# Reordering the first loads and splits, and the last squares and output tiles, of a hybrid RG-LRU and attention block in three-product fp32

## Chip, cores and metric

One core of one Trainium2 chip. The metric is the device time of one execution in microseconds; shorter is better. Three runs of the kernel before gave a median of 1032.5 us (1031.96 to 1032.81).

## What is computed

One layer on 1024 tokens of width 1024, in float32. Cut to what matters:

```python
h = rmsnorm(x, g_mix); z = h @ w_in                # 1024 x 1024 @ 1024 x 1792
lx, lg, q, k, v = split(z)
lx = causal_depthwise_conv(lx, w_conv, b_conv)
y_lru = rmsnorm(rg_lru(lx, ...) * gelu(lg), g_lru_out)
y_att = rmsnorm(chunk_window_attention(q, k, v, sinks), g_attn_out)
x = x + concatenate([y_lru, y_att]) @ w_out
x = x + square(relu(rmsnorm(x, g_ffn) @ w_ff1)) @ w_ff2     # width 4096
gate = sigmoid(rmsnorm(x, g_ple) @ w_ple_gate)
x = x + gate * (p @ w_ple_proj)
return rmsnorm(x, g_final)
```

## The kernel before

Everything is held transposed: channels on the 128 partitions, tokens along the free axis. xT is x as eight tiles of 128 channels (k = 0 to 7) by 1024 tokens, worked in two halves of 512 tokens (`half(0)`, `half(1)`). Each float32 operand of a matrix product is split into a rounded part (hi, made by ScalarE as a copy to fp32r) and a remainder (lo, by VectorE or GpSimd as a subtraction), and each product is three matmuls in a row, hi x hi (L815), lo x hi (L816), hi x lo (L817). The order of instructions is written out by hand for each engine, and semaphores join them. A wait stops its engine's whole queue.

**The head.** w_in is read in pieces of [2, 128, 1024]; a half piece `s` holds four k tiles of 256 columns. The first half piece (s = 0) is loaded in two parts: columns 0 to QP = 512 (L495, k = 0 and 1) and QP to HP = 1024 (L497, k = 2 and 3). SP issues, in this order: the first part (L495), the vectors (gains and biases, [128, 80], L496), the second part (L497), token tiles 2 and 3 (L499), then the half pieces s = 1, 2, 3 (L488) with pairs of token tiles (L481) between and behind them. ScalarE's own queue issues token tiles 0 and 1 (L1216, L1217) and then waits for constants and data. Semaphores: tile 0 `first_x_in`, tile 1 `x_in[0]`, tile 2 `x_in[1]`, tile 3 `third_x_in`, the second part `stage_in[0]`.

Splitting: VectorE makes h_hi of tile 0 (L1774, needs the vectors and tile 0), w_lo of the first part (L1776), h_lo of tiles 0 and 1 (`mix_low`, recorded at L1682), w_lo of the second part (L1785), h_lo of tile 2, the first sum of squares, h_lo of tile 3, and w_lo of s = 1 (L1691). ScalarE makes w_hi of the first part (L1221), h_hi of tile 1 (`mix_high`, recorded at L1192), w_hi of the second part (L1239), h_hi of tile 2, the square of tile 0 (L1197), h_hi of tile 3, w_hi of s = 1 (L1178), and so on. TensorE runs nine warming products (L968), then `first_half`: k = 0 in three steps of two columns blocks each (L846, L850, L854), k = 1 (needs h_lo of tile 1), k = 2 and 3 (need the second part's w_lo and their h_lo), then s = 1, 2, 3 in turn. Six matmuls belong to each k: two column blocks by three. The second token half follows from group 4 on, with the sums of squares (L881, L882) in the middle of its first group.

**The tail.** The last stage works in 20 cells (`CELLS`), q = 0 to 19: eight channel tiles by token parts, the last ones 256 tokens wide. For each, TensorE multiplies the gate (`gate`) and projects (`project`, both L815 to L817); VectorE multiplies by the norm (`gate_scale`, L2255), ScalarE takes the sigmoid (L1610), VectorE multiplies by the projection and adds to x (`gate_add`, L2269 and L2271), ScalarE squares (`final_square`, L1617), GpSimd sums (L798). Cells come in pairs; step q = 16 is cells 16 and 17, step 18 is cells 18 and 19. Between them VectorE writes finished output tiles, `out_tile(k, part)` at L2275 (part 0 is 512 tokens, parts 1 and 2 are 256 each; part 2 is the last), and SP stores them in pairs of k, waiting in order. For the last part ScalarE loads the table of the square root early by a tiny operation (L1640), squares cell 18 (`final_square(q - 1)`), scales tile 6 (`final_scale`, L1626), and takes two roots of column sums (L1651). TensorE's column sums (L1151) stand behind seven warming products (L1154) and read the running sum, the square of cell 18 and that of cell 19 (VectorE, L2314). Then VectorE inverts (L2319), makes two diagonals (L2322), TensorE spreads them (L1166), and the last tiles are multiplied (L2329, L807) and stored (L681, L1659).

Of the kernel before, what the change touches and what calls it, by code (L numbers as in the profile page):

```python
# [13 lines left out]
P = 128  # L14
SEQ = 1024
D = 1024
KD = D // P
# [102 lines left out]
def build(nc, x, p, vectors, gates_w, w_in, w_out, w_ff1, w_ff2, w_ple_gate, w_ple_proj, alibi, out):  # L120
    ctx = ExitStack()
    with ctx:
# [3 lines left out]
        def at(name, offset, shape, dt=F32):  # L126
            return nc.alloc_sbuf_tensor_at(name, shape, dt, offset=base + offset)

        def sem(name):
            return ctx.enter_context(nc.semaphore(name))  # L130
# [5 lines left out]
        xT = at("xT", XT, [P, KD, SEQ])  # L136
# [81 lines left out]
        for name, shape in (("r_mix", [P, SEQ]), ("ident", [P, P]), ("ones", [P, P]), ("vec", [P, NVEC]),  # L218
# [7 lines left out]
        r_mix, ident, ones, vec = (small[n] for n in ("r_mix", "ident", "ones", "vec"))  # L226
# [11 lines left out]
        x_in = [sem(f"x_in{i}") for i in range(8)]  # L238
        stage_in = [sem(f"stage_in{i}") for i in range(STAGES)]

        vec_in, gatew_in, bias_in, p_in = sem("vec_in"), sem("gatew_in"), sem("bias_in"), sem("p_in")
        pw_in, pw_high, pw_ready, pp_kept = sem("pw_in"), sem("pw_high"), sem("pw_ready"), sem("pp_kept")
        last_square = sem("last_square")
        first_w_in, first_x_in, third_x_in, last_done = (
            sem(n) for n in ("first_w_in", "first_x_in", "third_x_in", "last_done"))
# [44 lines left out]
        def half(hf):  # L290
            return slice(hf * HALF, (hf + 1) * HALF)
# [185 lines left out]
        def _(sp):  # L477
# [15 lines left out]


            sp.dma_start(stage[:, 0, 0:QP], w_in[0, 0, :, 0:QP]).then_inc(first_w_in, 16)  # L495
            sp.dma_start(vec[:, :], vectors).then_inc(vec_in, 16)  # L496
            sp.dma_start(stage[:, 0, QP:HP], w_in[0, 0, :, QP:HP]).then_inc(stage_in[0], 16)  # L497
            for k in (2, 3):
                sp.dma_start(xT[:, k, half(0)], x[k * P:(k + 1) * P, half(0)]).then_inc(  # L499
                    x_in[1] if k == 2 else third_x_in, 16)  # L500
            for s in range(1, 4):
                if s > 1:
                    load_x(s)
# [167 lines left out]
            for part in range(LAST):  # L671
                for pair in range(KD // 2):
                    k = 2 * pair
# [497 lines left out]
        def _(act):  # L1171
# [37 lines left out]
            def root(n, b, dst, width):  # L1209
# [3 lines left out]
                act.activation(dst[:, tok], bank[b][:, 0:cols], ACT.Sqrt, bias=eps[:, 0:1],  # L1213
                               scale=1.0 / width).then_inc(rms_done, 1)

            act.dma_start(xT[:, 0, half(0)], x[0:P, half(0)]).then_inc(first_x_in, 16)  # L1216
            act.dma_start(xT[:, 1, half(0)], x[P:2 * P, half(0)]).then_inc(x_in[0], 16)  # L1217
            act.wait_ge(consts, 3)
            act.activation(lam[:, 2, :], ones[:, 0:LT], ACT.Square)
            act.wait_ge(first_w_in, 16)  # L1220
# [3 lines left out]
            def mix_high(k, hf):  # L1224

                if (k % 2 == 0) if hf or k > 1 else (k == 1):
                    act.wait_ge(x_in[4 * hf + k // 2], 16)
                if hf == 0 and k == 3:
                    act.wait_ge(third_x_in, 16)
                split_high(H_MIX + KD * hf + k, xT[:, k, half(hf)], v_mix[:, k:k + 1], k, hf)  # L1230

            def mix_square(k, hf):

                square(KD * hf + k, sq, xT[:, k, half(hf)])

            act.wait_ge(h_high, H_MIX + 1)
            mix_high(1, 0)
            act.wait_ge(stage_in[0], 16)
            act.activation(w_hi[:, 0, QP:HP], stage[:, 0, QP:HP], ACT.Copy).then_inc(w_high, 1)  # L1239
            mix_high(2, 0)  # L1240
            mix_square(0, 0)
            mix_high(3, 0)
            high(1)
# [333 lines left out]
            def gate_high(n):  # L1577

                high(2 * n)
                high(2 * n + 1)  # L1580
# [31 lines left out]
            def final_square(q):  # L1612

                m, _, tok, _ = cell(q)
                act.wait_ge(x_gated, 2 * (q + 1))
                act.wait_ge(sq_used, SQ_BY[SS_FIN - 1] + q - 1)
                act.activation(cell_square(q), xT[:, m, tok], ACT.Square).then_inc(sq_done, 1)  # L1617
# [10 lines left out]
            for q in range(len(CELLS)):  # L1628
                if q in (14, 17):
                    root(SS_FIN + (q == 17), 4, r_fin, D)  # L1630
                sigmoid(q)
                if q == 0:
                    total_head(SS_PLE + 1)
                if q == 3:
                    root(SS_PLE + 1, 4, r_mix, D)
                if q in (5, 7):
                    act.wait_ge(gate_done, q + 1)
                    gate_high(GATE_FIRST + 2 + (q == 7))
                if q == len(CELLS) - 1:
                    act.activation(lam[:, 2, :], ones[:, 0:LT], ACT.Sqrt)  # L1640
                    final_square(q - 1)
                    final_scale(KD - 2)
                elif q % 2 == 1:
                    final_square(q - 1)
                    final_square(q)
                if 16 <= q < 19:
                    for k in (2 * (q - 16), 2 * (q - 16) + 1):
                        final_scale(k)
# [15 lines left out]
        def _(dve):  # L1664
# [113 lines left out]
            def mix_low(k, hf):  # L1778

                split_low(H_MIX + KD * hf + k, xT[:, k, half(hf)], v_mix[:, k:k + 1], k, hf)  # L1780

            mix_low(0, 0)
            mix_low(1, 0)
            dve.wait_ge(w_high, 1)
            dve.tensor_tensor(w_lo[:, 0, QP:HP], stage[:, 0, QP:HP], w_hi[:, 0, QP:HP], ALU.subtract  # L1785
                              ).then_inc(w_split, 1)
            mix_low(2, 0)
            add_square(dve, SS_MIX, 0, sq, acc)
            mix_low(3, 0)
            w_low(1)  # L1790
# [482 lines left out]
            def out_tile(k, part):  # L2273

                dve.scalar_tensor_tensor(out=result(k, part), in0=xT[:, k, tokens(part)], scalar=v_fin[:, k:k + 1],  # L2275
                                         in1=r_fin[:, tokens(part)], op0=ALU.mult, op1=ALU.mult
                                         ).then_inc(out_ready[k], 1)

            for q in range(0, len(CELLS), 2):
                gate_scale(q)  # L2280
                if q == 0:
                    for i in range(6, KD):
                        ple_low(i, 1)
                if q == 14:
                    invert(SS_FIN, r_fin)
                if q == 16:
                    for k in (2, 3, 4):
                        out_tile(k, 0)
                if q == 18:
                    for k in (6, 7):  # L2290
                        out_tile(k, 0)
                    for k in (0, 1):
                        out_tile(k, 1)
                gate_scale(q + 1)
                if q == 16:
                    invert(SS_FIN + 1, r_fin)
                gate_add(q)
                gate_add(q + 1)
                if q == 2:
                    invert(SS_PLE + 1, r_mix)  # L2300
                if q in (4, 6):
                    for h in range(2):
                        w_low(2 * (GATE_FIRST + 2 + (q == 6)) + h)
                if q == 14:
                    for k in (0, 1):
                        out_tile(k, 0)
                if q == 16:
                    out_tile(5, 0)

            q = len(CELLS) - 1  # L2310
# [1 line left out]
            dve.wait_ge(x_gated, 2 * (q + 1))  # L2312
            dve.wait_ge(sq_used, SQ_BY[SS_FIN - 1] + q - 1)
            dve.tensor_tensor(cell_square(q), x_last, x_last, ALU.mult).then_inc(last_square, 1)  # L2314
            for k in range(2, KD - 2):
                out_tile(k, 1)
            dve.wait_ge(rms_done, SS_FIN + LAST + LAST_HALVES)
            columns = lam[:, 3, 0:LAST_HALVES]
# [70 lines left out]
```

## Time and profile before

| | us |
|---|---|
| median of three runs | 1032.5 (1031.96 to 1032.81) |
| the profiled execution | 1032.53 |
| its span | 1030.7 |
| TensorE matmul busy | 1021.3 (99%) |
| VectorE busy | 765.9 (74%) |
| ScalarE busy | 526.5 (51%) |
| GpSimd busy | 500.1 (49%) |

The span is the time between the first and the last instruction or transfer of the profile; the execution's own time is 1.8 us more. Busy shares are of the span. TensorE's granted clock is 0.998 of full over the span. Times in the rows below are microseconds from the span's start.

### The profile page before, as it was taken

What the parts mean: (1) busy time and instruction counts of PE and PEld (TensorE: products, weight loads), DVE (VectorE), ACT (ScalarE), POOL (GpSimd) and SP (SyncE); (2) the same over time, 40 slices, a digit from 0 to 9 for tenths busy, and PEclk for the clock granted to TensorE, in tenths of its full rate; (3) what the DMA queues carried; (4) which work ended last, traced back from release to release, by engine and by line L of the source; (5) the groups of instructions that cost most, each with busy time, mean ns of one, the idle gap of its engine ahead of it and who ended that gap; (6) DMA issues with size and microseconds to landing.
All of it is one profiled execution on the core that took longest, in us unless ns stands there. A gap on an engine that the chain in (4) does not pass through costs nothing.

```text
span 1030.7 us, 13984 instructions
## 1 busy us (share of the span) xinstructions
PE 1021.3 (99%) x4780; PEld 836.0 (81%) x4780; DVE 765.9 (74%) x906; ACT 526.5 (51%) x940; POOL 500.1 (49%) x350
## 2 busy tenths in 40 slices
PE   9999999999999999999999999999999999999997
PEld 7877788777888788888888888888888888888897
DVE  7988787888798777787787787866776765754658
ACT  7557755655677534334334355443455453653334
POOL 0000052343304887887887657445557555741221
PEclk9999999999999999999999999999999999999999
DMA  9101102102003666767867699668985664600004
GB/s 346 44 26 57 41 0 93 41 10 69 6 1 133 248 236 249 273 245 259 280 240 260 242 350 325 194 215 286 313 262 175 192 198 150 220 1 1 1 1 164
DMA packets 63972, 166.15 MB, mean 161 GB/s; under 512 B 6960, under 2 KB 9008, under 8 KB 61872
## 3 DMA queue, kind: packets, MB, share of 16 engines
q1 hardware_dynamic: 63088, 164.43, 46.2%
q10 hardware_dynamic: 832, 1.05, 0.3%
q8 instruction: 30, 0.49, 0.2%
q14 instruction: 22, 0.18, 0.1%
HBM read 115.12 MB, written 50.33 MB: 161 GB/s over the span
## 4 chain that ended last, share of the span: by engine, by line
PE 92%; DVE 5%; issue 1%; ACT 1%; DMA 1%; SPq 0%; DVEq 0%; ACTq 0%
PE bank L815 30%; PE bank L816 29%; PE bank L817 29%; PE bank L930 1%; PE bank L960 1%; DVE h_lo L1984 1%; PE bank L901 1%; PE bank L945 1%; DVE r_ffn L1696 1%; DMA stage<-in_w_in 1%; DVE t_lo L2076 0%; DVE acc L465 0%; ACT t_hi L1475 0%; PE bank L885 0%; DVE w_lo L1691 0%
## 5 line engine op out<-in xcount | busy, mean ns | idle before, releaser
L815 PE MATMUL bank<-h_hi,w_hi 128*128 128x512 f32 (+1 forms) x574 | 220.9, 385 | 0.6 <-DVE h_lo L1682 0.5
L816 PE MATMUL bank<-h_lo,w_hi 128*128 128x512 f32 (+1 forms) x574 | 217.0, 378 | 0.0
L817 PE MATMUL bank<-h_hi,w_lo 128*128 128x512 f32 (+1 forms) x574 | 216.9, 378 | 0.0
L773 POOL TENSOR_TENSOR left_lo<-left_raw,left_hi 128x512 fp32r<-128x512 f32 x88 | 125.7, 1436 | 104.7 <-ACT left_hi L1531 104.1
L2153 DVE TENSOR_TENSOR right_lo<-right_raw,right_hi 128x512 fp32r<-128x512 f32 x88 | 117.4, 1347 | 56.7 <-ACT right_hi L1532 56.6
L815 PE MATMUL bank<-right_hi,left_hi 128*128 128x512 f32 x352 | 136.9, 389 | 0.0
L817 PE MATMUL bank<-right_hi,left_lo 128*128 128x512 f32 x352 | 136.9, 389 | 0.0
L816 PE MATMUL bank<-right_lo,left_hi 128*128 128x512 f32 x352 | 136.9, 389 | 0.0
L815 PEld LDWEIGHTS bank<-h_hi,w_hi 128*128 128x128 f32 x574 | 108.0, 188 | 28.9 <-issue 6.2
L817 PEld LDWEIGHTS bank<-h_hi,w_lo 128*128 128x128 f32 x574 | 108.0, 188 | 20.4
L816 PEld LDWEIGHTS bank<-h_lo,w_hi 128*128 128x128 f32 x574 | 108.1, 188 | 19.6 <-issue 0.5
L1531 ACT ACTIVATE left_hi<-left_raw 128x512 fp32r<-128x512 f32 x88 | 55.5, 631 | 111.2 <-DMA right_raw<-u_b 62.9
L745 POOL TENSOR_TENSOR slot_lo<-w_raw,slot_hi 128x512 fp32r<-128x512 f32 x56 | 78.6, 1405 | 24.0 <-ACT slot_hi L1494 23.7
L815 PE MATMUL bank<-h_hi,slot_hi 128*128 128x512 f32 x224 | 87.7, 392 | 0.9 <-DVE u L2114 0.9
L2089 DVE TENSOR_TENSOR w_set<-w_set 128x512 f32<-128x512 f32 x52 | 76.2, 1465 | 14.9 <-DMA w_set<-in_w_ff 14.0
L817 PE MATMUL bank<-h_hi,slot_lo 128*128 128x512 f32 x224 | 87.2, 389 | 0.0
L816 PE MATMUL bank<-h_lo,slot_hi 128*128 128x512 f32 x224 | 87.2, 389 | 0.0
L817 PEld LDWEIGHTS bank<-right_hi,left_lo 128*128 128x128 f32 x352 | 66.1, 188 | 13.8
L815 PEld LDWEIGHTS bank<-right_hi,left_hi 128*128 128x128 f32 x352 | 66.1, 188 | 13.8
L816 PEld LDWEIGHTS bank<-right_lo,left_hi 128*128 128x128 f32 x352 | 66.1, 188 | 13.6
L745 POOL TENSOR_TENSOR slot_lo<-s_raw,slot_hi 128x512 fp32r<-128x512 f32 x42 | 60.1, 1446 | 20.2 <-ACT slot_hi L1494 18.3
L817 PE MATMUL bank<-t_hi,slot_lo 128*128 128x512 f32 x168 | 65.4, 389 | 0.0
(250 smaller groups left out, 2031.9 us busy)
## 6 DMA issues: line engine op xcount, KB each, us to landing
w_raw<-in_w_ff SPq DMA_DIRECT2D x28, 512.0 KB, 5.4
right_raw<-u_b SPq DMA_DIRECT2D x56, 256.0 KB, 4.3
w_set<-in_w_ff SPq DMA_DIRECT2D x26, 512.0 KB, 5.9
w_sums<-w_set SPq DMA_DIRECT2D x13, 1024.0 KB, 3.9
left_raw<-w_sums SPq DMA_DIRECT2D x48, 256.0 KB, 3.9
left_raw<-in_w_ff SPq DMA_DIRECT2D x40, 256.0 KB, 3.0
u_b<-u SPq DMA_DIRECT2D x16, 512.0 KB, 3.0
u_t<-usq SPq DMA_DIRECT2D x16, 512.0 KB, 6.4
```

The source lines that it names most:

```text
L745: pool.tensor_tensor(slot_lo[i], w1_left(raw, i), slot_hi[i], ALU.subtract).then_inc(w1_split, 1)
L773: pool.tensor_tensor(left_lo[o][:, :], left_raw[o][:, :], left_hi[o][:, :], ALU.subtract).then_inc(left_ready, 1)
L815: pe.matmul(o, whi, hh, start=first, stop=False, skip_group_check=onto)
L816: pe.matmul(o, whi, hl, start=False, stop=False, skip_group_check=onto)
L817: return pe.matmul(o, wlo, hh, start=False, stop=last, skip_group_check=onto)
L901: last = pe.matmul(bank[4 + 2 * hf + i][gate_block(i, n), :], gate_w[block, i, j, block], yl(j)[block, half(hf)], start=True, stop=True)
L930: last = pe.matmul(bank[4 + g][:, (2 * cp + a) * P:(2 * cp + a + 1) * P], qT[r, c, 2 * a:2 * a + 2, :].rearrange("p a q -> p (a q)"), kT[r ...
L945: last = pe.transpose(bank[6 + g][:, i * P:(i + 1) * P], prob[:, u % 2, (4 * g + i) * P:(4 * g + i + 1) * P], ident[:, :])
L960: last = pe.matmul(bank[3][g * HD:(g + 1) * HD, cp * 256:(cp + 1) * 256], v[:, c, g * HD:(g + 1) * HD], probT[:, g * 512 + cp * 256:g * 51 ...
L1531: act.activation(left_hi[o][:, :], left_raw[o][:, :], ACT.Copy).then_inc(left_high, 1)
L2089: dve.tensor_tensor(out, one, other, op).then_inc(made, 1)
L2153: dve.tensor_tensor(right_lo[o][:, :], right_raw[o][:, :], right_hi[o][:, :], ALU.subtract).then_inc(right_ready, 1)
```

## The change

Four moves. The count of operations, transfers and bytes stays.

1. The vectors' load goes from SP's second place to the first place of ScalarE's queue. Token tile 0 is second there. Token tile 1 moves to SP's second place, and tile 2 to SP's third, ahead of the second part of the first half piece, which is now fourth; tile 3 stays fifth.
2. ScalarE rounds tile 2 ahead of the second part of the weights, and VectorE makes tile 2's remainder ahead of that part's.
3. The square of cell 18 stands ahead of the operation that loads the square root's table.
4. Of the output tiles, tile 6 of part 0 moves from step 18 to step 16, and tile 2 of part 1 from behind the last square to step 18.

```diff
--- before.py
+++ after.py
@@ -493,11 +493,10 @@
 
 
             sp.dma_start(stage[:, 0, 0:QP], w_in[0, 0, :, 0:QP]).then_inc(first_w_in, 16)
-            sp.dma_start(vec[:, :], vectors).then_inc(vec_in, 16)
+            for k, arrived in ((1, x_in[0]), (2, x_in[1])):
+                sp.dma_start(xT[:, k, half(0)], x[k * P:(k + 1) * P, half(0)]).then_inc(arrived, 16)
             sp.dma_start(stage[:, 0, QP:HP], w_in[0, 0, :, QP:HP]).then_inc(stage_in[0], 16)
-            for k in (2, 3):
-                sp.dma_start(xT[:, k, half(0)], x[k * P:(k + 1) * P, half(0)]).then_inc(
-                    x_in[1] if k == 2 else third_x_in, 16)
+            sp.dma_start(xT[:, 3, half(0)], x[3 * P:4 * P, half(0)]).then_inc(third_x_in, 16)
             for s in range(1, 4):
                 if s > 1:
                     load_x(s)
@@ -1213,8 +1212,8 @@
                 act.activation(dst[:, tok], bank[b][:, 0:cols], ACT.Sqrt, bias=eps[:, 0:1],
                                scale=1.0 / width).then_inc(rms_done, 1)
 
+            act.dma_start(vec[:, :], vectors).then_inc(vec_in, 16)
             act.dma_start(xT[:, 0, half(0)], x[0:P, half(0)]).then_inc(first_x_in, 16)
-            act.dma_start(xT[:, 1, half(0)], x[P:2 * P, half(0)]).then_inc(x_in[0], 16)
             act.wait_ge(consts, 3)
             act.activation(lam[:, 2, :], ones[:, 0:LT], ACT.Square)
             act.wait_ge(first_w_in, 16)
@@ -1235,9 +1234,9 @@
 
             act.wait_ge(h_high, H_MIX + 1)
             mix_high(1, 0)
+            mix_high(2, 0)
             act.wait_ge(stage_in[0], 16)
             act.activation(w_hi[:, 0, QP:HP], stage[:, 0, QP:HP], ACT.Copy).then_inc(w_high, 1)
-            mix_high(2, 0)
             mix_square(0, 0)
             mix_high(3, 0)
             high(1)
@@ -1637,8 +1636,8 @@
                     act.wait_ge(gate_done, q + 1)
                     gate_high(GATE_FIRST + 2 + (q == 7))
                 if q == len(CELLS) - 1:
+                    final_square(q - 1)
                     act.activation(lam[:, 2, :], ones[:, 0:LT], ACT.Sqrt)
-                    final_square(q - 1)
                     final_scale(KD - 2)
                 elif q % 2 == 1:
                     final_square(q - 1)
@@ -1781,10 +1780,10 @@
 
             mix_low(0, 0)
             mix_low(1, 0)
+            mix_low(2, 0)
             dve.wait_ge(w_high, 1)
             dve.tensor_tensor(w_lo[:, 0, QP:HP], stage[:, 0, QP:HP], w_hi[:, 0, QP:HP], ALU.subtract
                               ).then_inc(w_split, 1)
-            mix_low(2, 0)
             add_square(dve, SS_MIX, 0, sq, acc)
             mix_low(3, 0)
             w_low(1)
@@ -2284,12 +2283,11 @@
                 if q == 14:
                     invert(SS_FIN, r_fin)
                 if q == 16:
-                    for k in (2, 3, 4):
+                    for k in (2, 3, 4, 6):
                         out_tile(k, 0)
                 if q == 18:
-                    for k in (6, 7):
-                        out_tile(k, 0)
-                    for k in (0, 1):
+                    out_tile(7, 0)
+                    for k in (0, 1, 2):
                         out_tile(k, 1)
                 gate_scale(q + 1)
                 if q == 16:
@@ -2312,7 +2310,7 @@
             dve.wait_ge(x_gated, 2 * (q + 1))
             dve.wait_ge(sq_used, SQ_BY[SS_FIN - 1] + q - 1)
             dve.tensor_tensor(cell_square(q), x_last, x_last, ALU.mult).then_inc(last_square, 1)
-            for k in range(2, KD - 2):
+            for k in range(3, KD - 2):
                 out_tile(k, 1)
             dve.wait_ge(rms_done, SS_FIN + LAST + LAST_HALVES)
             columns = lam[:, 3, 0:LAST_HALVES]
```

## Rows read from the trace of the kernel before

**Rows 1.** The page, part 4: shares of the chain that ended last, by engine.
```profile
PE 92%; DVE 5%; issue 1%; ACT 1%; DMA 1%; SPq 0%; DVEq 0%; ACTq 0%
```

**Rows 2.** TensorE's waits in the whole span: in total, times, longest us.
```profile
PE bank L815 <- DVE u L2114: 0.9, 1, 0.9
```

**Rows 3.** Chain that ended last, 0 to 13 us: start, us, what.
```profile
1.68 5.56 DMA stage<-in_w_in
...
7.27 0.64 ACT w_hi L1239
...
7.93 0.69 DVE w_lo L1785
...
8.64 0.76 DVE h_lo L1682
...
9.54 0.47 PE bank L815
10.02 0.23 PE bank L816
```

**Rows 4.** DMA issues, one at a time: KB each, us from issue to landing.
```profile
xT<-in_x ACTq DMA_DIRECT2D x1, 256.0 KB, 3.6
...
vec<-in_vectors SPq DMA_DIRECT2D x1, 40.0 KB, 3.7
...
xT<-in_x ACTq DMA_DIRECT2D x1, 256.0 KB, 4.4
...
stage<-in_w_in SPq DMA_DIRECT2D x1, 256.0 KB, 5.6
...
stage<-in_w_in SPq DMA_DIRECT2D x1, 512.0 KB, 6.7
```

**Rows 5.** DMA view, 0 to 14 us: rate in 40 slices of 0.35 us.
```profile
GB/s 0 0 0 0 0 82 222 380 363 365 369 259 190 193 176 228 298 375 421 398 392 421 410 415 392 386 369 351 357 369 415 427 404 386 421 421 433 427 392 392
```

**Rows 6.** Timeline of the two issuing queues: start, us, queue, line, transfer.
```profile
1.20 0.46 ACTq L1217 DMA_DIRECT2D xT<-in_x  x1
...
2.15 0.91 SPq L499 DMA_DIRECT2D xT<-in_x  x2
```

**Rows 7.** Timeline, 4 to 13 us: start, us, engine, line, out<-in, [idle before <-releaser].
```profile
4.92 0.49 DVE L1774 TENSOR_SCALAR h_hi<-xT,vec 128x512 fp32r<-128x512 f32 x1 [3.90 <-DMA vec<-in_vectors]
...
5.92 1.41 DVE L1682 SCALAR_TENSOR_TENSOR h_lo<-xT,vec,h_hi 128x512 fp32r<-128x512 f32 x2
...
9.85 1.06 ACT L1178 ACTIVATE w_hi<-stage 128x1024 fp32r<-128x1024 f32 x1
...
11.02 1.23 DVE L1691 TENSOR_TENSOR w_lo<-stage,w_hi 128x1024 fp32r<-128x1024 f32 x1 [0.49 <-ACT w_hi L1178]
...
12.37 0.43 PE L815 MATMUL bank<-h_hi,w_hi 128*128 128x512 f32 x1
```

**Rows 8.** VectorE's timeline, and the chain (TensorE), where k = 7 nears.
```profile
32.02 0.73 DVE L1682 SCALAR_TENSOR_TENSOR h_lo<-xT,vec,h_hi 128x512 fp32r<-128x512 f32 x1
...
33.95 0.23 PE bank L817
```

**Rows 9.** Chain that ended last, from 1019 us on: start, us, what.
```profile
1020.24 1.56 PE bank L1154 x14
1021.80 1.15 PE bank L1151 x10
...
1022.97 0.48 ACT lam L1651 x2
```

**Rows 10.** Timeline of VectorE and ScalarE, 1020 to 1023 us; columns as in rows 7.
```profile
1020.14 0.42 DVE L2271 TENSOR_TENSOR xT<-xT,gt 128x256 f32<-128x256 f32 x1
...
1020.25 1.28 ACT L1640 ACT_TABLE_LOAD   x1
...
1021.65 0.40 ACT L1617 ACTIVATE sq<-xT 128x256 f32<-128x256 f32 x1
1022.09 0.51 ACT L1626 ACTIVATE xT<-xT,vec 128x256 f32<-128x256 f32 x1
```

**Rows 11.** VectorE's timeline in step 18: two long and two short output tiles.
```profile
1017.10 2.35 DVE L2275 SCALAR_TENSOR_TENSOR xT<-xT,vec,r_fin 128x512 f32<-128x512 f32 x4
```

## The prediction

> **What bounds the kernel now.** I read the page first: the chain that ended last lies on TensorE for 92% of the span, on VectorE for 5% [rows 1]. The kernel is a stream of matrix products that hardly ever stops. So I asked for TensorE's waits in the whole span: after the first 10 us the only ones that the view names are 0.9 us in the feed-forward part, which is fed by TensorE's own products [rows 2], and one in the last 8 us. Whatever the change gains must come from before the stream is dense or from behind its end, where the edits lie. It can be worth tenths of a microsecond.
>
> The head is read in the chain of its first 13 us [rows 3]. The chain is: the load of the second piece (columns QP to HP of the first half of w_in's first piece), issued at 1.68 and landed at 7.24; ScalarE's rounding, 0.64; VectorE's remainder, 0.69; VectorE's h_lo of token tile 2, 0.76; TensorE at 9.54. Both tile 2 and the piece are needed for the products of k = 2. TensorE then runs k = 2 and 3 (twelve products at 0.23) and meets a second gate: the next half piece, L1178 to L1691, lets it go on at 12.37 [rows 7]. From there it runs through.
>
> The tail is TensorE's too: seven warming products (14 records), the column sums, and only then ScalarE's two roots at 1022.97 [rows 9].
>
> **The head, part by part.** Call H the start of VectorE's first operation, L1774, which needs the vectors and token tile 0. It is 4.92, and the vectors are what it waited for [rows 7]. Behind it VectorE runs without a gap to the end of h_lo of tile 1 at 5.92 + 1.41 = 7.33, which is H + 2.41 [rows 7]. TensorE's six products of k = 1 take 0.47 + 5 x 0.23 = 1.62 [rows 3]. So TensorE could begin k = 2 at H + 4.05 = 8.97 with 0.02 for the hand-over, and begins at 9.54: **0.57 us is the stall that the second piece causes**.
>
> 1. Order of tile 2 and the piece. Tile 2's rounding (ScalarE) and h_lo (VectorE) go ahead of the piece. If both have landed in time, VectorE's chain ends at 7.33 + 0.76 + 0.69 = 8.78 for the old H, below 8.97: the stall goes, and what is late next is VectorE's chain from H itself. The edit puts ScalarE's wait for tile 2 ahead of the piece's rounding; queued behind it are that rounding, L1197 and tile 3. TensorE needs both before k = 2, so a late tile costs the difference between it and the piece only.
>
> 2. Queues. SP issues every 0.47 us. Its second place goes from the vectors (40 KB) to tile 1, the third from the piece to tile 2, the fourth (2.15 [rows 6]) to the piece, the fifth stays with tile 3. ScalarE's queue has the vectors at 0.75 and tile 0 at 1.20, the place that tile 1 had [rows 6]. Issue counts stay, and GpSimd's instructions and queue are untouched. The vectors took 3.7 from issue, so they land near 0.75 + 3.7 = 4.45, and H now hangs on tile 0. Bounds: it took 3.6 when it was first in the queue, giving 4.8; tile 1, second in the same queue behind a full tile, took 4.4, giving 5.6 [rows 4]. Tile 0 will stand second, but behind 40 KB instead of 256 KB, so I take 5.05 as an estimate between them: **H is 0.13 later**.
>
> 3. The next half piece. It is the fifth load behind the first of SP and took 6.7 us from its issue [rows 4]; ScalarE takes it at 9.85, and TensorE gets it 2.52 us later, at 12.37 [rows 7]. All that is ahead of it is the same number of bytes, so the question is how well the DMA engines are filled. The rate line has a hollow: six slices of 0.35 us (from 3.85 us on) at 259 to 298, while later ones stand near 390 GB/s [rows 5]. The hollow misses (131 + 200 + 197 + 214 + 162 + 92) x 0.35 us = 0.35 MB, or 0.9 us at 390 GB/s. It begins when the vectors are being written through SP's queue, and the load behind them took 5.6 where those ahead took 3.6 [rows 4]. If small rows in SP's queue make the hollow, SP's stream is free of it now and the half piece comes up to 0.9 earlier; if the hollow is only the start of the DMA engines, nothing moves. I take about half, 0.5: forecast landing 9.3 where it was 9.83.
>
> **The Trainium skill beside it.** The trace shows the load behind the vectors landing 2.34 us after them (7.24 against 4.90). The skill's page "DMA: Bandwidth & Descriptors" (Specifications) wants transfers of at least 512 B for the line rate; a row of the vectors is 80 numbers, 320 B. By that rule the small rows, now ahead of tile 0 in one queue, slow what stands behind them; that is the third rival, priced from rows below.
>
> **The sum.** TensorE passes the second gate at the later of H + 4.05 + 12 x 0.228 = H + 6.79 and the half piece's handling + 2.52. With H = 5.05 the first is 11.84; with a landing at 9.3 (taken up 0.02 later, as before) the second is 11.84 as well. Against 12.37 the gain is **0.53 us**. It must survive to the end. The nearest thing behind the gate is k = 7 of group 4: VectorE's h_lo is done at 32.75, TensorE wants it at 34.18 [rows 8], a slack of 1.4, more than the gain even if VectorE does not move. Behind that every wait of TensorE is for work that its own products started, so it shifts along.
>
> **The tail.** The out tiles: one long one (512 columns) goes from step 18 to step 16, where it fills an idle stretch before TensorE's next result, and a short one (tile 2 of part 1) comes from behind the last square to step 18. Four tiles, two long and two short, took 2.35 [rows 11], that is 0.39 for 256 columns, so VectorE reaches its last gate_scale 0.39 earlier. Its next operation needs TensorE's projection, which ends 6 products of 0.12 before 1020.24, at 1019.52, so the last adds come 0.1 to 0.2 earlier. ScalarE: the square of cell 18 waits for the add that ended at 20.56 (1020.14 + 0.42 [rows 10]). It then runs 0.40, the table 1.28, the small root (0.12 to the next start) and the scaling (0.51) [rows 10]: 1020.60 + 0.40 + 1.28 + 0.12 + 0.51 = 1022.91 at the old time of the add, 1022.75 with the earlier add. The root is wanted at 1022.97, when TensorE's tenth column record ends. TensorE is busy without a gap from 1020.24 until then [rows 9], and its two reads of that square follow one another; so neither the earlier square nor the tile taken from behind the last square shortens anything: **0.0**, bounds -0.1 (the square was just in time at 22.05 and may have held one record) and +0.1 (the margin of 0.06 is used up). What hides the moved table is TensorE's warming and sums; without that cover its 1.28 would count. The stores of part 1 leave up to 0.4 earlier, but the last store hangs on the roots.
>
> Forecast: the profiled execution took 1032.53 with a span of 1030.7, so 1.8 us lie around it; it equals the median of 1032.5. 1032.53 - 0.53 = **1032.0**.
>
> **Rivals.**
> - A. The places hold: each load lands when the load in its place did. The piece, at 2.15, lands 5.6 later at 7.75, is rounded and split (0.64 + 0.69) by 9.1; TensorE may start k = 2 0.3 earlier, but the half piece is where it was and gives it all back at 12.37. Time 1032.5. For it: from 5.6 us on the rate is full, so landing goes by bytes. Against: the hollow.
> - B. Slower: tile 0 is late behind the vectors. The load behind the vectors landed 2.34 us after them. Applied to ScalarE's queue: 4.45 + 2.34 = 6.8 = H, the gate opens at 13.6, **+1.2**: 1033.7. It turns to a loss from H = 5.58 on. Against it: the hollow may be of both queues, and tile 0 is the only load there, while the piece had SP's stream and tile 1 beside it.
> - C. The tail gives too: if the last square's reads did hold TensorE, or the stores' earlier end frees the last ones, 0.3 more: 1031.7.
> - D. The table. In the trace ScalarE's load of the root's table takes 1.28 and the next operation begins 0.01 later [rows 10]. The skill's page "ScalarE: Activation LUTs" (What ACT_TABLE_LOAD costs) adds a drain of about 1.38 us to each switch. As a mechanism of this kernel: an added pause as long as the load itself (1.28) behind it would put the roots at 22.91 + 1.28 = 24.2, +1.2: 1033.7. The rows leave no room for it before the change (21.53 to 21.65), so 0.01.
>
> **How the numbers follow.** Forecast 0.46 (its own range 1031.6 to 1032.3), A 0.28, B 0.13, C 0.07, D 0.01, and 0.05 for something that the trace doesn't show (a different meeting of DMAs in the streamed part), half of it either way. The three runs lie 0.85 apart, so 0.3 of noise is added at both ends. From C's 1031.7 and a landing 0.9 earlier (H at 4.8: 0.78) down, 1031.2; up to A with noise, 1032.9; left out are most of B, D and the unknown. A measurement of this kernel can tell about 0.2%, 2.1 us, from no change. No named case reaches that: same 0.94, faster 0.03, slower 0.03, all from the unknown and its like.
>
> **What would show it.** Right: L1774 released by tile 0 at 5.0 to 5.2; tile 2's h_lo ahead of the piece's remainder; no wait of 0.5 on h_lo before 10 us; the half piece's rounding near 9.3; the first product behind the second gate near 11.8; in the tail ScalarE idle for 0.0 to 0.2 before the roots and TensorE's last sums as long after its last projection as now. Wrong: L1774 after 5.6 (B); L1178 still at 9.85 (A); the roots earlier relative to the projections (C); a pause behind the table (D); a difference of over 2 us, which would have to appear in the streamed part.

## The result, and the profile after

The changed kernel took 1033.78 us (median of 22 runs, 1032.63 to 1035.83), the kernel before 1032.2 (22 runs, 1031.79 to 1032.96) beside it. The ratio is 1.0014, with a 95% interval of 1.0008 to 1.0019: **1.6 us slower** where 0.5 faster was forecast, and above the stated range. By the bound of 0.2% it is still no change. The spread grew from 1.2 to 3.2 us. The times stand in groups: 8 runs up to 1033.2 (median 1032.87), 10 from 1033.7 to 1034.3, 4 from 1034.5 on.

The profiled execution took 1033.83 (before 1032.53), its span is 1032.0 (before 1030.7). The shares of the chain hardly moved against [rows 1]:

```profile
PE 92%; DVE 5%; ACT 1%; issue 1%; DMA 0%; ACTq 0%; DVEq 0%
```

The head tells it. Timeline of the changed kernel, 0 to 14 us (start, us, engine, line, out<-in, idle before and its releaser); it answers to [rows 6, 7]:

```profile
1.14 4.21 PE L967 MATMUL bank<-ones 128*128 128x128 f32 x18 [1.14 <-POOL eps L690]
1.20 0.90 SPq L497 DMA_DIRECT2D xT<-in_x  x2
1.21 0.45 ACTq L1216 DMA_DIRECT2D xT<-in_x  x1
...
6.14 0.49 DVE L1773 TENSOR_SCALAR h_hi<-xT,vec 128x512 fp32r<-128x512 f32 x1 [5.13 <-DMA xT<-in_x]
...
6.78 1.19 PE L845 MATMUL bank<-h_hi,w_hi 128*128 128x512 f32 x2 [1.43 <-DVE h_hi L1773]
...
9.47 0.63 PE L814 MATMUL bank<-h_hi,w_hi 128*128 128x512 f32 x1
...
9.62 1.04 ACT L1177 ACTIVATE w_hi<-stage 128x1024 fp32r<-128x1024 f32 x1
...
9.90 0.52 PE L815 MATMUL bank<-h_lo,w_hi 128*128 128x512 f32 x1
10.26 0.39 PE L816 MATMUL bank<-h_hi,w_lo 128*128 128x512 f32 x1
...
13.93 0.39 PE L814 MATMUL bank<-h_hi,w_hi 128*128 128x512 f32 x1
```

Token tile 0 releases VectorE's first operation at 6.14; before, the vectors released it at 4.92. TensorE, whose warming products end at 5.35, sits idle for 1.43 us, and when it starts, its products lie 0.43 apart (9.47, 9.90) until about 10.2, and 0.23 after that; before, they were 0.23 apart from k = 1 on. The product behind the second gate (the wait for the next half piece of w_in) starts at 13.93 instead of 12.37: 1.56 late. The half piece was not in the way, its rounding began at 9.62.

The DMA issues one at a time (KB, us from issue to landing), which answer to [rows 4]:

```profile
vec<-in_vectors ACTq DMA_DIRECT2D x1, 40.0 KB, 3.3
...
xT<-in_x SPq DMA_DIRECT2D x1, 256.0 KB, 4.7
...
xT<-in_x ACTq DMA_DIRECT2D x1, 256.0 KB, 4.8
...
stage<-in_w_in SPq DMA_DIRECT2D x1, 256.0 KB, 5.4
```

The vectors land at 4.05, tile 1 (SP's second) at 5.9, tile 0 (ScalarE's second) at 6.05, the second weight part at 7.5.

The tail, which answers to [rows 9, 10]. First TensorE's closing warming products in the timeline of the kernel before:

```profile
1020.08 1.73 PE L1154 MATMUL bank<-ones 128*128 128x128 f32 x14
```

Then those of the changed kernel, and ScalarE behind them:

```profile
1021.50 1.73 PE L1153 MATMUL bank<-ones 128*128 128x128 f32 x14
...
1021.96 0.42 ACT L1616 ACTIVATE sq<-xT 128x256 f32<-128x256 f32 x1 [0.58 <-DVE xT L2270]
1022.39 1.28 ACT L1640 ACT_TABLE_LOAD   x1
1023.69 0.20 ACT L1640 ACTIVATE lam<-ones 128x4 f32<-128x4 f32 x1
1023.80 0.49 ACT L1625 ACTIVATE xT<-xT,vec 128x256 f32<-128x256 f32 x1
1024.27 0.48 ACT L1650 ACTIVATE lam<-bank,eps 128x1 f32<-128x1 f32 x2
```

ScalarE now runs from the square to the roots without a gap. The roots begin 2.77 us after the first closing warming product (1021.50 to 1024.27), before 2.89 (1020.08 to 1022.97): **the tail gained 0.12**.

### The profile page after: what moved, and what is told of

Read it like the earlier page. It is cut to its first block, busy times and chain, and to the rows that moved or that the text cites. A ratio compares the mean times of both kernels' runs of the same rounds, so it can differ in the third digit from the quotient of the medians.

```text
span 1032.0 us, 13984 instructions
## 1 busy us (share of the span) xinstructions
PE 1021.9 (99%) x4780; PEld 837.4 (81%) x4780; DVE 766.0 (74%) x906; ACT 526.0 (51%) x940; POOL 499.4 (48%) x350
## 4 chain that ended last, share of the span: by engine, by line
PE 92%; DVE 5%; ACT 1%; issue 1%; DMA 0%; ACTq 0%; DVEq 0%
PE bank L814 30%; PE bank L815 29%; PE bank L816 29%; PE bank L929 1%; PE bank L959 1%; DVE h_lo L1983 1%; PE bank L900 1%; PE bank L944 1%; DVE r_ffn L1695 1%; DMA xT<-in_x 0%; DVE t_lo L2075 0%; DVE acc L465 0%; ACT t_hi L1474 0%; PE bank L884 0%; DVE w_lo L1690 0%
```

## The experiments

Theory at this point: (1) tile 0 is late because it stands second in ScalarE's queue, behind the vectors; (2) the idle stretch of TensorE costs as much again through its clock; (3) the tail is a small gain. The rival to (1) is that SP's full tiles in the first microseconds make ScalarE's loads late, whatever their order; the rival to (2) is that lateness is all.

### Head and tail apart

`tail_only` is the kernel before with the tail's hunks of the diff alone; `head_only` is the changed kernel with these undone.

```diff
                 if q == len(CELLS) - 1:
+                    final_square(q - 1)
                     act.activation(lam[:, 2, :], ones[:, 0:LT], ACT.Sqrt)
-                    final_square(q - 1)
...
-                    for k in (2, 3, 4):
+                    for k in (2, 3, 4, 6):
                         out_tile(k, 0)
...
-            for k in range(2, KD - 2):
+            for k in range(3, KD - 2):
```

> The kernel before with the tail's edits alone (square of cell 18 ahead of the table, the two output tiles moved). In the changed kernel's profile TensorE's first read of that square starts 0.36 us after the sums' start where it was 0.47 before, and ScalarE is the last to be ready. Theory (the tail gives 0.1): roots begin 0.1 us earlier relative to the end of the last projection, time 0.1 below the kernel before. Rival (the tail costs, because the table now stands behind the square): roots 0.1 or more later. If the whole loss came from the tail, this kernel would be 1.5 slower.

Measured: 1031.91 (11 runs) against 1032.27, ratio 0.9996 (0.9987 to 1.0005). Its profile:

```profile
1019.57 1.73 PE L1154 MATMUL bank<-ones 128*128 128x128 f32 x14
...
1022.34 0.49 ACT L1651 ACTIVATE lam<-bank,eps 128x1 f32<-128x1 f32 x2
```

2.77 us again. The 0.12 is in both profiles with this tail; the time, 0.36 lower, agrees in sign but its interval holds zero.

> The changed kernel with the tail of before. Theory (the head costs all of it: token tile 0, second in ScalarE's queue behind the vectors, lands near 6.0 and TensorE starts 1.2 us later, at half its clock until near 10): 1.6 to 1.7 us slower than the kernel before, with runs spread over 2 us or more. Rival (head and tail disturb each other): no slower than 1.0.

Measured: 1034.12 against 1032.27, ratio 1.0013 (1.0004 to 1.0022), 1032.77 to 1034.7. The head costs all of it. The profiled execution was one of the quick group, 1032.80: VectorE's first operation at 6.01, TensorE idle for 1.29, and yet its products were 0.23 apart from the start of k = 1 on, and the roots came 2.89 after the warming, as before. So lateness and slow products are two things. (The expectation had put slow products into this profile; they were not in it.)

### Is the slow stretch the clock, and what is it worth?

```diff
-WARM, WARM_END = 9, 7
+WARM, WARM_END = 12, 7
```

> The changed kernel with 12 warming products instead of 9, which keeps TensorE busy until 6.6 us, about when its first operand is there. Theory (two costs: 0.5 to 0.6 for the late token tile, 1.0 for products at half the clock after the idle 1.4 us): full clock from near 5.7 us on, second gate near 12.9 where it was 13.9, time 1.0 below the changed kernel, 0.4 to 0.5 above the kernel before. Rival (the clock costs nothing of its own, the lateness is all): as the changed kernel.

Measured: 1032.89 against 1032.27 for the kernel before, ratio 1.0006 (0.9997 to 1.0015); ten of eleven runs lie between 1032.64 and 1033.09. With this the upper groups are gone but for one run. Profile:

```profile
6.27 0.49 DVE L1773 TENSOR_SCALAR h_hi<-xT,vec 128x512 fp32r<-128x512 f32 x1 [5.25 <-DMA xT<-in_x]
...
6.90 0.47 PE L845 MATMUL bank<-h_hi,w_hi 128*128 128x512 f32 x1 [0.33 <-DVE h_hi L1773]
...
12.94 0.39 PE L814 MATMUL bank<-h_hi,w_hi 128*128 128x512 f32 x1
```

Tile 0 is as late as in the changed kernel, even later by 0.13, but TensorE passes the second gate at 12.94, not 13.93. Against that profile three extra products that compute nothing give back 1.0 us, and the median is 0.9 lower than the changed kernel's 1033.78 (the two intervals, each against the kernel before, overlap). What is left against the kernel before, 0.6, is lateness.

The converse: the kernel before with too short a warming, its data being early.

```diff
-WARM, WARM_END = 9, 7
+WARM, WARM_END = 6, 7
```

> The kernel before with 6 warming products instead of 9, so that TensorE is idle for 1.5 us ahead of its first real product, as in the changed kernel, while all data come as early as before. Theory (the idle stretch by itself can delay the step to the full clock): in some or all executions the products run at 0.42 instead of 0.23 us apiece until near 9 or 10 us, part of it hidden behind the second weight part: 0.3 to 1.0 slower than the kernel before, with a wider spread. Rival (the idle stretch costs nothing where data are on time): the same time and spread as before.

Measured: 1032.92 against 1032.31, ratio 1.0004 (0.9995 to 1.0013), 1032.37 to 1033.6. Profile (1033.16):

```profile
5.02 1.19 PE L846 MATMUL bank<-h_hi,w_hi 128*128 128x512 f32 x2 [0.94 <-DVE h_hi L1774]
...
10.15 0.40 PE L815 MATMUL bank<-h_hi,w_hi 128*128 128x512 f32 x1
...
12.88 0.39 PE L815 MATMUL bank<-h_hi,w_hi 128*128 128x512 f32 x1
```

The vectors happened to land early here (first product at 5.02), so the idle stretch was 0.94 and not the 1.5 aimed at. Still the second gate is passed at 12.88 instead of 12.37, since the products are slow up to about 10. A short warming costs 0.5 to 0.6 here without any late data. In this execution it cost more: the half piece was rounded at 9.49, 0.36 earlier than in the profile before, and with the 2.52 of the prediction the gate would have been passed at 12.01 (an estimate), not 12.88. The interval of the time holds zero, so the cost rests on the profile's products.

### Why is tile 0 late?

ScalarE's two loads swapped, SP's order kept:

```diff
-            act.dma_start(vec[:, :], vectors).then_inc(vec_in, 16)
             act.dma_start(xT[:, 0, half(0)], x[0:P, half(0)]).then_inc(first_x_in, 16)
+            act.dma_start(vec[:, :], vectors).then_inc(vec_in, 16)
```

> The changed kernel with the two loads of ScalarE's queue swapped: token tile 0 first, the vectors second. SP's order stays. Theory (the place behind the vectors is what makes tile 0 late): tile 0 lands near 4.4, the vectors near 4.9, first operation of VectorE near 4.9, second gate at 11.8 to 12.1, time 0.3 to 0.6 below the kernel before, spread as small as before. Rival (SP's third full tile in the first microseconds makes ScalarE's loads late, whatever their order): tile 0 still later than 5.3 and the kernel no faster than the one before.

Measured: 1033.99 against 1032.27, ratio 1.0014 (1.0005 to 1.0023): as slow as the changed kernel. The theory as I had put it here (the place behind the vectors) fell; of the rival one half came, a kernel no faster, and the other, tile 0 itself later than 5.3, did not.

```profile
xT<-in_x ACTq DMA_DIRECT2D x1, 256.0 KB, 3.5
...
vec<-in_vectors ACTq DMA_DIRECT2D x1, 40.0 KB, 4.8
...
6.04 0.49 DVE L1773 TENSOR_SCALAR h_hi<-xT,vec 128x512 fp32r<-128x512 f32 x1 [5.03 <-DMA vec<-in_vectors]
```

Tile 0 lands at 4.25, but now the vectors, 40 KB, take 4.8 us from the second place and land at 6.0, just where tile 0 landed before the swap. What stands second in ScalarE's queue is late, be it large or small, with small or large rows ahead of it.

SP held back until tile 0 is there:

```diff
+            sp.wait_ge(first_x_in, 16)
             for k, arrived in ((1, x_in[0]), (2, x_in[1])):
```

> The changed kernel, but SP issues nothing behind the first weight part until token tile 0 has landed. Theory (tile 0 is late because a full tile of SP's queue, issued at the same moment, fills the same DMA engines, and landing goes by bytes in both queues): tile 0 lands between 4.4 and 5.0. Rival (the second place in ScalarE's queue is late whatever SP does): tile 0 lands near 6.0 again. The rest of the loads comes later by design, so the time will be 1 to 3 above the kernel before, which says nothing of either.

```profile
xT<-in_x ACTq DMA_DIRECT2D x1, 256.0 KB, 3.3
...
4.63 0.49 DVE L1774 TENSOR_SCALAR h_hi<-xT,vec 128x512 fp32r<-128x512 f32 x1 [3.62 <-DMA xT<-in_x]
```

Still second behind the vectors, tile 0 now takes 3.3 us instead of 4.8 and lands at 4.5. **What made it late is SP's loads issued beside it.** They were all held back together, so this run doesn't say which of them does it. The profiles of the other runs say a part. In `order_and_tail` (below) SP's second place has the 40 KB of vectors again, as before, and its third place a full tile. The second load of ScalarE's queue, tile 1, took nearly as long there:

```profile
xT<-in_x ACTq DMA_DIRECT2D x1, 256.0 KB, 4.7
```

With the vectors in SP's second place, ScalarE's second load took 4.0 to 4.7 us in five profiles (`short_warm`, `tail_only`, `tail_shorter`, the kernel before, `order_and_tail`). With a full tile there it took 4.7 to 5.9 in the seven profiles that keep its issue at 1.20. The two ranges touch: the full tile in the place of the vectors makes it later on the whole, but how much of the lateness is its own is open. (The whole took 1035.63 against 1032.31, ratio 1.0029, 1.0018 to 1.0040, because the other loads now start at 4.54.)

The small rows doubled: the vectors in two loads of 40 columns, and the two waits for them raised to 32.

```diff
-            act.dma_start(vec[:, :], vectors).then_inc(vec_in, 16)
+            for o in (slice(0, NVEC // 2), slice(NVEC // 2, NVEC)):
+                act.dma_start(vec[:, o], vectors[:, o]).then_inc(vec_in, 16)
```

> The changed kernel with the vectors loaded as two loads of 40 columns each, ahead of tile 0 in ScalarE's queue: the same 40 KB in 256 rows of 160 B, and one issue more. Theory (bytes in both queues decide, small rows do not): tile 0 lands within 0.4 of the changed kernel's 6.05, most of that from its issue 0.45 later. Rival (small rows ahead of it make tile 0 late): it lands later by 0.8 or more, and the second gate with it.

```profile
xT<-in_x ACTq DMA_DIRECT2D x1, 256.0 KB, 4.6
...
6.38 0.49 DVE L1774 TENSOR_SCALAR h_hi<-xT,vec 128x512 fp32r<-128x512 f32 x1 [5.37 <-DMA xT<-in_x]
...
7.02 0.70 PE L845 MATMUL bank<-h_hi,w_hi 128*128 128x512 f32 x2 [1.67 <-DVE h_hi L1774]
```

Twice the rows of half the size, and tile 0 takes 4.6 from an issue 0.47 later: 0.24 later than in the changed kernel, less than its issue. The small rows are not the cause. TensorE was idle for 1.67 here, longer than in the changed kernel, and its products ran 0.23 apart. The time was 1035.84 (6 runs) against 1032.31, ratio 1.0033 (1.0020 to 1.0045), although the profiled execution, the lowest of the six, took 1033.61; why most executions were 2 us above that one the single profile doesn't tell.

### The parts of the head apart

`queues_only` is the kernel before with the vectors and tile 0 in ScalarE's queue and tile 1 in SP's second place; the second weight part stays ahead of tile 2, and the splits and the tail are those of before.

```diff
-            sp.dma_start(vec[:, :], vectors).then_inc(vec_in, 16)
+            sp.dma_start(xT[:, 1, half(0)], x[P:2 * P, half(0)]).then_inc(x_in[0], 16)
             sp.dma_start(stage[:, 0, QP:HP], w_in[0, 0, :, QP:HP]).then_inc(stage_in[0], 16)
...
+            act.dma_start(vec[:, :], vectors).then_inc(vec_in, 16)
             act.dma_start(xT[:, 0, half(0)], x[0:P, half(0)]).then_inc(first_x_in, 16)
-            act.dma_start(xT[:, 1, half(0)], x[P:2 * P, half(0)]).then_inc(x_in[0], 16)
```

> The kernel before with the loads' places alone changed: the vectors and tile 0 from ScalarE, tile 1 second from SP where the vectors were; the second weight part third, tile 2 fourth, the order of the splits and the tail as before. Theory (these places are the whole loss): tile 0 lands near 6.0, first operation of VectorE 1.1 to 1.3 later, 0.6 to 1.9 slower than the kernel before with the two groups of times that the changed kernel shows. Rival (tile 2's place, or the changed order of the splits, is part of the loss): less than 0.5 slower.

Measured: 1034.84 against 1032.38, ratio 1.0024 (1.0015 to 1.0033), 1034.27 to 1035.95. The places alone cost 2.5 us, more than the whole change (1.6) and more than the 1.9 that the expectation allowed.

```profile
7.24 0.49 DVE L1774 TENSOR_SCALAR h_hi<-xT,vec 128x512 fp32r<-128x512 f32 x1 [6.22 <-DMA xT<-in_x]
...
7.87 0.70 PE L846 MATMUL bank<-h_hi,w_hi 128*128 128x512 f32 x2 [2.53 <-DVE h_hi L1774]
```

Tile 0 lands at 7.1 here, and TensorE is idle for 2.5 us. This profile also has the granted clock in its rows. By stretches (us, TensorE busy, granted clock, DMA share, GB/s):

```profile
8.70:11.90 3.20, 3.20 (x9) 0.50 1.00 369
12.10:14.00 1.90, 1.90 (x10) 1.00 1.03 412
```

and two products of the first stretch in its timeline:

```profile
10.51 0.63 PE L816 MATMUL bank<-h_lo,w_hi 128*128 128x512 f32 x1
10.93 0.63 PE L817 MATMUL bank<-h_hi,w_lo 128*128 128x512 f32 x1
```

Granted 0.50 of full, that is 1.2 GHz, the products are 0.42 apart; at 1.00, 2.4 GHz, 0.23. Here the first products ran at full rate (0.70 for two), and the clock fell near 8.6, behind the idle stretch of 2.53 and 0.7 us of products. The changed kernel shows the same pair of distances, but its rows list the granted clock of the slow stretch as full:

```profile
6.80:9.90 3.10, 3.10 (x7) 1.00 1.03 381
```

The column can't be taken at its word there: it reads 1.00 over the head's warming products too, though 18 of their records take 4.21 us, and 14 like them in the tail take 1.73. That the slow products of the changed kernel ran at the lower level is therefore read from their distance alone.

`order_and_tail` keeps the places of before, with only tile 2's load ahead of the second weight part's, and has the changed order of the splits and the changed tail. Against the changed kernel:

```diff
-            for k, arrived in ((1, x_in[0]), (2, x_in[1])):
-                sp.dma_start(xT[:, k, half(0)], x[k * P:(k + 1) * P, half(0)]).then_inc(arrived, 16)
+            sp.dma_start(vec[:, :], vectors).then_inc(vec_in, 16)
+            sp.dma_start(xT[:, 2, half(0)], x[2 * P:3 * P, half(0)]).then_inc(x_in[1], 16)
...
-            act.dma_start(vec[:, :], vectors).then_inc(vec_in, 16)
             act.dma_start(xT[:, 0, half(0)], x[0:P, half(0)]).then_inc(first_x_in, 16)
+            act.dma_start(xT[:, 1, half(0)], x[P:2 * P, half(0)]).then_inc(x_in[0], 16)
```

> The queues of before (tiles 0 and 1 from ScalarE, the vectors second from SP), only token tile 2 ahead of the second weight part; splits in the changed order; the tail of the changed kernel. Theory (the loss is the late start of VectorE, which the vectors' and tile 1's new places cause; the order of tile 2 and the part is harmless or good): first operation of VectorE near 4.9 as before, second gate at 11.9 to 12.4, roots 0.12 earlier than before relative to the projections, time 0.1 to 0.6 below the kernel before and spread below 1.5. Rival (the order costs): at least 0.3 slower.

Measured: 1032.33 against 1032.31, ratio 0.9999 (0.9990 to 1.0009).

```profile
4.96 0.49 DVE L1773 TENSOR_SCALAR h_hi<-xT,vec 128x512 fp32r<-128x512 f32 x1 [3.95 <-DMA vec<-in_vectors]
...
9.03 0.45 PE L814 MATMUL bank<-h_hi,w_hi 128*128 128x512 f32 x1
...
11.98 0.50 PE L814 MATMUL bank<-h_hi,w_hi 128*128 128x512 f32 x1
```

The order does what it is for: k = 2 starts at 9.03, without the stall of 0.57. But the half piece lets TensorE on at 11.98 only, 2.48 behind its landing at 9.5. `tail_only`, with the loads and splits of before, got the half piece at 9.5 too:

```profile
9.52 1.06 ACT L1178 ACTIVATE w_hi<-stage 128x1024 fp32r<-128x1024 f32 x1
...
12.07 0.40 PE L815 MATMUL bank<-h_hi,w_hi 128*128 128x512 f32 x1
```

So between these two profiles the order is worth 0.1 at the gate, and the rest is given back there; the medians show no gain of it. The loss is all in the places of the vectors and of tiles 0 and 1.

### How much of the spread is the landing?

`changed_again` and `queues_again` are second profiles of two kernels, one execution each.

> A second profile of the changed kernel, to see what of its spread comes from the loads. Theory (tile 0's landing is a property of the queues, the spread is the clock's): tile 0 lands within 0.3 of 6.05 again, and the full clock begins near 5.7 or near 10. Rival (the landing itself varies from run to run by 1 us): it lands before 5.5 or after 6.6.

```profile
6.17 0.49 DVE L1773 TENSOR_SCALAR h_hi<-xT,vec 128x512 fp32r<-128x512 f32 x1 [5.16 <-DMA xT<-in_x]
...
6.80 0.70 PE L845 MATMUL bank<-h_hi,w_hi 128*128 128x512 f32 x2 [1.45 <-DVE h_hi L1773]
...
12.87 0.39 PE L814 MATMUL bank<-h_hi,w_hi 128*128 128x512 f32 x1
```

1032.84 us. Tile 0 is as late and the idle stretch as long (1.45) as in the first profile, but the first two products take 0.70 instead of 1.19, and the gate is passed at 12.87 instead of 13.93. Same landing, 1.06 apart at the gate and 0.99 in time: **with the same late landing the products can be slow or not, and that is worth 1.0 us**. The two profiles fall into the two lower groups of times. That these groups are the two behaviours is likely but rests on one profile of each; and three of the ten executions of the middle group list a mean granted clock of 0.996, as the profile of `queues_only` does, so a clock that falls may be among them.

> A second profile of the kernel with the places of the loads alone, where tile 0 landed at 7.1. Theory (with the weight part instead of tile 2 in SP's third place, tile 0 lands 1 us later than in the changed kernel, in every run): near 7.1 again. Rival (chance of the run): near 6.0.

1034.68 us; tile 0 took 5.2 and landed at 6.4, between the two expectations. TensorE was idle for 1.97, and the granted clock fell to 0.50 here too (8.7 to 11.4 us). So the landing too moves by 0.7 from run to run when the queues stand this way. Whether the weight part in SP's third place has a share in it, two profiles don't settle.

### A version that uses the tail's gain

The kernel before with the changed tail, fewer closing warming products and the scaling of tile 6 behind the roots:

```diff
-WARM, WARM_END = 9, 7
+WARM, WARM_END = 9, 3
...
-                    final_scale(KD - 2)
...
+            final_scale(KD - 2)
             final_scale(KD - 1)
```

> The head of before and the tail of the changed kernel, with 3 instead of 7 warming products ahead of the column sums and the scaling of tile 6 behind the roots. Theory (since the square stands ahead of the table, TensorE's warming products and ScalarE's scaling end last together ahead of the roots): the roots begin 0.3 to 0.4 us earlier relative to the end of the last projection than in the kernel with the tail's edits alone, time 0.4 to 0.5 below the kernel before. Rival (TensorE falls to half its clock or waits for the last square, and gives it back): no faster than the kernel with the tail's edits alone.

Measured: 1031.94 against 1032.38, ratio 0.9996 (0.9986 to 1.0005).

```profile
1019.39 0.83 PE L1154 MATMUL bank<-ones 128*128 128x128 f32 x6
...
1021.70 0.40 ACT L1650 ACTIVATE lam<-bank,eps 128x1 f32<-128x1 f32 x2
```

The roots begin 2.31 after the warming, 0.46 earlier than with seven products; the profiled execution took 1031.24, 0.65 less than that of `tail_only`, but 0.44 of this is the head's scatter (second gate at 11.63 and 12.07). The medians are 0.44 and 0.36 (`tail_only`) below the kernel before, so the further 0.46 of the profile isn't seen in them. Neither version is shown to be faster than the kernel before.

## Why the prediction was wrong, point by point

- **H, the landing of tile 0: the step that failed.** I put it between 4.8 and 5.6 and took 5.05; tile 0 landed at 6.05 and H was 6.14, outside both bounds. I took 3.85 us from issue, below the 4.4 of the second place, because only 40 KB stood ahead in the same queue. What stands ahead made no difference that the runs show: the second load took 4.8 behind 40 KB, and 4.8 behind 256 KB in `tile_first`. I left out what SP issues beside it, where the same edit puts a full tile in the place of the 40 KB, with another behind it. `tile_alone` shows what SP's loads cost: 3.3 us without them, 4.8 with them. The upper bound of 4.4 was besides one execution's figure; with the vectors still in SP's second place, other profiles have 4.0 to 4.7.
- **The slow products: a term that was missing.** "H + 6.79" holds when the products run at 0.23: 12.96 is what it gives for the second profile's 6.17, and 12.87 was measured; 13.06 and 12.94 with the longer warming. In the first profile it misses by 1.0 (12.93 and 13.93). The idle stretch between the warming and the first product grew from 0.20 to 1.43, as it must with a late H, and I didn't ask what it does to the products behind it. Of the 1.56 at the second gate in the first profile 0.56 is lateness and 1.0 is slow products.
- **Rival B** had the right sign, place and turning point (a loss from H = 5.58 on) at a chance of 0.13. That its time, 1033.7, is within 0.1 of the measured 1033.78 is luck: its H of 6.8 was 0.65 too large, and the slow products, which it doesn't have, made up for it. Its reason was wrong: neither `tile_first` nor `vectors_halved` supports small rows. The 512 B of the Trainium skill's page ("DMA: Bandwidth & Descriptors", Specifications), on which the rival leaned, may hold for bandwidth; for the landing behind such rows doubling them showed nothing. Nearer to the matter is what the same page says under "Queues, rings and completion order": the two issuing engines' queues are rings on the same 16 DMA engines. The runs agree: 3.3 against 4.8 us.
- **The order of tile 2 and the weight part**: the stall goes as forecast, in `order_and_tail` k = 2 starts at 9.03 where H + 4.05 gives 9.01. It is worth 0.1 at the gate in one pair of profiles, because of the next step.
- **The half piece, and rival A** (the places hold, all is given back there): forecast to be taken at 9.32, it was taken at 9.62 in the changed kernel and at 9.53 in `order_and_tail`. But it was taken at 9.52 in `tail_only` and at 9.09 in `tail_shorter` too, with the loads in the old order, against 9.85 in the profile before. The 0.3 lies within the scatter of one order of loads and is no effect of the vectors' place; half of the forecast gain rested on one profile's landing.
- **The loss passes through**: of the 1.56 at the second gate 1.42 are left at the closing warming and 1.3 in the span. That step held, as did the slack.
- **The tail**: forecast 0.0 with bounds of 0.1, measured 0.12, just outside, rival C in small. TensorE's first read of the square had been held by 0.12 (22.05 against its turn), as the bound said. The table behind the square costs no pause (1023.67 to 1023.69), so rival D fell; the drain that the page "ScalarE: Activation LUTs" of the Trainium skill adds to a switch is in none of these rows.
- **Range and chances**: the range ended at 1032.9 and missed. The chance of no change by 0.2% (0.94) held, at a ratio of 1.0014.

## What to carry to other kernels

Read the first microseconds over all issuing queues together: a load's landing depends on what the other queues have under way, so a bound for a moved load must come from a row with the same neighbours, not only the same place in its own queue, and from more than one execution. Of the orders run here, that of the kernel before, with tile 0 first in ScalarE's queue and the 40 KB of vectors second in SP's, starts VectorE at 4.4 to 5.0 us; the orders with a full tile in that place of SP's start it at 6.0 to 7.2. And when the first real product can come later, let the warming products reach up to it: three that compute nothing took up to 1.0 us off an execution here, and the slow products behind an idle stretch cost more (1.0) than the lateness itself (0.6).

## What the runs showed of the hardware

- With SP's full tiles beside it, a load in the second place of ScalarE's queue took 4.8 us whether it had 256 KB or 40 KB; with nothing of SP's issued until it had landed, except the first load, 256 KB took 3.3. Over the profiles this place took 4.0 to 4.7 with 40 KB second in SP's queue, and 4.7 to 5.9 with 256 KB there.
- After an idle stretch of 1.43 to 1.45 us on TensorE the products ran at 0.43 apart until about 10.2 us in one execution and at 0.23 in the other, with the same landings: 1.0 us of difference between two executions of one kernel.
- The length of the idle stretch alone doesn't sort them: behind 0.76 (`tail_shorter`), 1.29 (`head_only`), 1.45 and 1.67 us (`vectors_halved`) the first products ran at full rate, behind 0.94 (`short_warm`), 1.32 (`tile_first`) and 1.43 they were slow.
- The products can be slow without any idle stretch too, if they come early: in `tile_alone` the first two started at 5.26 us, right behind the warming products, and took 1.19; the next two, at 6.25, took 0.70. So the slow stretch of the changed kernel can be read as the slow rate of the warming products lasting to 10.2 us.
- After idle stretches of 2.53 and 1.97 us the first products ran at full rate, and then the granted clock fell to 0.50: from 8.7 to 11.9 us in the one, from 8.7 to 11.4 in the other.
- The granted clock of the profile reads 1.00 over slow products in the head that no full-rate stretch preceded: the distance of the products tells there, not the column.
- With an idle stretch of 0.33 (longer warming), ten of eleven times lay within 0.5 us; without it the same kernel spread over 3.2.
